# Value slabs first, query and key slabs in pairs behind them: one edit to the head of a two-block transformer kernel

## The chip, the cores and the metric

The kernel runs on one core of a Trainium2 chip. The metric is the device time of one execution in microseconds (us), as the median of several runs. The core has five engines: TensorE (PE, matmuls), VectorE (DVE), ScalarE (ACT), GpSimd (POOL) and SyncE (SP). Each works through its own instruction stream in order and waits on semaphores for the others. SyncE and ScalarE also issue DMAs, each on its own queue.

## The reference

Two transformer blocks in fp32 on 512 tokens of 1024 features. What matters here is the first block's head: a norm, one wide projection, and its retention half.

```python
h = rmsnorm(x, norm_mix[l])
p = h @ w_in[l]
y_ret = retention_mixer(p[..., :RET_PROJ], ...)      # q, k, v, gate: 512 columns each
y_rwkv = rwkv7_mixer(p[..., RET_PROJ:], ...)

def retention_mixer(p, positions, gn_w, gn_b):
    q, k, v, g = jnp.split(p, 4, axis=-1)
    q = rope(q.reshape(B, S, RET_HEADS, HEAD_DIM), positions)
    k = rope(k.reshape(B, S, RET_HEADS, HEAD_DIM), positions) * (HEAD_DIM ** -0.5)
    y = retention_chunkwise(q, k, v)                 # 8 heads of 64
    return silu(g) * head_group_norm(y, gn_w, gn_b, GN_EPS_RET)
```

## The kernel before, in words

**Slabs.** All weights are cut into slabs of 128 x 1024 values (512 KB). Slab `s` is loaded into `w_raw`, four slots used in turn; SyncE issues the load of slab s + 4 when slab s is done. ScalarE copies it to a rounded `w_hi` (`split_hi`), GpSimd takes the rest, `w_lo = w_raw - w_hi`, and TensorE makes three matmuls for each product: high by high, high by low, low by high. `w_hi` has two slots, so the split of slab s + 2 waits until slab s is done. The input `x` is split in the same way into `a_hi` (ScalarE) and `a_lo` (VectorE), eight feature tiles of 128 (index `kc`).

**Two kinds of slab.** A feature slab (`slab`, L1388 ff.) holds 128 output features over all eight `kc`: 24 matmuls of 128 x 512 into one PSUM bank, banks 0 and 1 in turn. It may begin when the tile two slabs back has been taken out of its bank (`begin`, semaphore `tile_taken`). A value slab (`wide`) holds two `kc` of all 512 value features: also 24 matmuls, twelve for each `kc`, into four banks with tokens on the partitions. Its sums are complete with the fourth of them only.

**Order before.** Slabs 0 to 3 are the query tiles, 4 to 7 the key tiles (`S_RQ`, `S_RK`), 8 to 11 the values (`S_RV`), 12 and on (`S_WA`) the second mixer's projections. Only slab 0 waits for `a_lo` piece by piece. Behind slab 0 TensorE sums the squares of `x` over the features (L1482, L1484: two fp32 matmuls with a tile of ones); ScalarE takes the root, VectorE the reciprocal `rstd`, with which every tile is multiplied when it is taken. Behind slab 4 eight tiny matmuls (L1487) turn `rstd` into a column for the value tiles.

**What a query or key tile needs.** VectorE takes tile j (`qk <- banks, rstd`). ScalarE issues four DMAs that copy it with its halves swapped into `rot` (`swap_halves`). VectorE makes three pieces of `rope`: `tmp <- rot, sin`, `qk <- qk, cos`, `qk <- qk, tmp`. ScalarE copies two halves rounded (`ret_hi`, into `q_twice` or `k_stack`), VectorE subtracts them (`ret_lo`, into `q_low` or `qk_lo`), and ScalarE issues two DMAs that stack the halves on the other partitions (`ret_stack`). In the loops over slabs, at slab s VectorE does: take s, `rope(s - 1)`, `ret_lo(s - 3)`. ScalarE does: `split_hi(s + 2)`, `swap_halves(s)`, `ret_hi(s - 3)`, `ret_stack(s - 4)`. During slabs 8 to 11 VectorE takes nothing until all four are done; it finishes `rope(7)` and the last `ret_lo` there and then takes four value tiles.

**The heads.** Behind each of slabs 12 to 19 TensorE computes `scores(h)` of one head; `scores(h)` for h >= 1 waits until VectorE has multiplied the scores of head h - 1 by the decay (`masked_scores`, tile `s_ret`). Head 0 waits for all eight tiles to be stacked. Behind heads 2, 4, 6 the outputs of a pair of heads are formed (`ret_out`, L1431). The decay table (2 MB) is loaded by a DMA of ScalarE's queue at slab 8.

The instruction streams are written out by hand in these loops; nothing else orders them. The lines L831 to L868 and L401, L338 are helpers that record VectorE's, ScalarE's and GpSimd's pieces.

## Time and profile before

| what | value |
|---|---|
| time, median of 3 runs | 1326.78 us (1326.47 to 1327.30) |
| the profiled execution: its time, its span | 1326.74 us, 1325.0 us |
| TensorE busy in the span | 1264.7 us, 95% |
| VectorE, ScalarE, GpSimd busy | 711.0, 545.7, 533.5 us |
| mean granted clock of TensorE | 0.987 |
| TensorE busy in the first 43.6 us | 29.5 us |
| TensorE busy from 43.6 to 110.2 us | 64.8 us |

The span runs from the first to the last instruction of the profiled execution. "Granted clock" is the share of TensorE's full 2.4 GHz that it was given; its other level is 1.2 GHz, shown as 0.50. A matmul's end is modelled in the profile, so the distance between two starts tells its pace better than its length. The releaser of a wait is inferred from semaphore events.

### The profile page before, as it was taken

How to read it: one execution, taken by the hardware profiler on the slowest of the kernel's cores; microseconds unless marked ns; L12 is line 12 of the kernel's file. 1: busy time of each engine (PE TensorE's matmuls, PEld its weight loads, DVE VectorE, ACT ScalarE, POOL GpSimd, SP SyncE). 2: the span in 40 equal slices, each digit the busy share in tenths (PEclk: the TensorE clock that was granted, in tenths of full speed). 3: DMA queues.
4: the chain of work that ended last, by engine and by line, in shares of the span. 5: the costliest groups of instructions: out<-in, count | busy, mean ns of one | idle time of the engine just before them, and what ended most of it. 6: DMA issues, size and time to landing. Idle time of an engine off the chain costs nothing.

```text
span 1325.0 us, 20731 instructions
## 1 busy us (share of the span) xinstructions
PE 1264.7 (95%) x8300; PEld 1003.5 (76%) x8300; DVE 711.0 (54%) x827; ACT 545.7 (41%) x734; POOL 533.5 (40%) x245
## 2 busy tenths in 40 slices
PE   5999999888899999999999999999999999999995
PEld 3777757677777877788888888888776777777873
DVE  8788756757559533336224143144477755442833
ACT  5332253244253433543223122235332468885342
POOL 4443222710157742274444444445443332223453
PEclk9999999989899999999999999999999999999998
DMA  6571111110045221122223332222422322112221
GB/s 218 160 229 64 64 48 53 59 35 4 12 158 163 100 78 51 48 96 96 95 95 96 101 102 100 96 96 96 144 88 80 108 75 65 64 65 67 99 90 64
DMA packets 35098, 119.91 MB, mean 91 GB/s; under 512 B 4544, under 2 KB 4672, under 8 KB 34624
## 3 DMA queue, kind: packets, MB, share of 16 engines
q1 hardware_dynamic: 29808, 105.78, 24.0%
q10 hardware_dynamic: 5200, 12.85, 3.1%
q8 instruction: 66, 1.08, 0.3%
q14 instruction: 24, 0.20, 0.1%
HBM read 111.01 MB, written 2.10 MB: 85 GB/s over the span
## 4 chain that ended last, share of the span: by engine, by line
PE 78%; DVE 14%; ACT 4%; issue 2%; ACTq 1%; DMA 1%; POOL 0%; DVEq 0%; SPq 0%
PE banks L1383 20%; PE banks L1385 19%; PE banks L1384 19%; DVE y_mid L831 2%; DVE tmp L831 1%; PE banks L1846 1%; PE banks L1404 1%; PE banks L1862 1%; PE banks L1406 1%; PE banks L1405 1%; PE banks L1951 1%; DVE qk L831 1%; PE banks L1936 1%; PE banks L1611 1%; DVE yk L831 1%
## 5 line engine op out<-in xcount | busy, mean ns | idle before, releaser
L338 POOL TENSOR_TENSOR w_lo<-w_raw,w_hi 128x1024 fp32r<-128x1024 f32 x145 | 353.7, 2440 | 536.9 <-ACT w_hi L401 536.7
L401 ACT ACTIVATE w_hi<-w_raw 128x1024 fp32r<-128x1024 f32 x145 | 153.9, 1062 | 333.2 <-PE banks L1385 213.1
L1383 PE MATMUL banks<-a_hi,w_hi 128*128 128x512 f32 x584 | 235.2, 403 | 15.5 <-DVE a_lo L839 13.4
L1385 PE MATMUL banks<-a_hi,w_lo 128*128 128x512 f32 x616 | 241.1, 391 | 0.0
L1384 PE MATMUL banks<-a_lo,w_hi 128*128 128x512 f32 x584 | 228.5, 391 | 0.0
L1385 PE MATMUL banks<-b_hi,w_lo 128*128 128x512 f32 x384 | 149.5, 389 | 0.0
L1383 PEld LDWEIGHTS banks<-a_hi,w_hi 128*128 128x128 f32 x584 | 110.1, 188 | 50.2 <-issue 17.8
L1385 PEld LDWEIGHTS banks<-a_hi,w_lo 128*128 128x128 f32 x616 | 116.2, 189 | 24.9
L831 DVE TENSOR_TENSOR x_res<-banks,x_res 128x512 f32<-128x512 f32 x56 | 38.7, 692 | 178.5 <-PE banks L1385 178.3
L338 POOL TENSOR_TENSOR w_lo<-w_raw,w_hi_mlp 128x1024 fp32r<-128x1024 f32 x36 | 87.3, 2425 | 107.7 <-ACT w_hi_mlp L401 107.7
L1384 PEld LDWEIGHTS banks<-a_lo,w_hi 128*128 128x128 f32 x584 | 110.3, 189 | 21.6 <-issue 0.7
L1383 PE MATMUL banks<-b_hi,w_hi 128*128 128x512 f32 x256 | 101.5, 396 | 0.0
L1384 PE MATMUL banks<-b_lo,w_hi 128*128 128x512 f32 x256 | 99.6, 389 | 0.0
L1385 PE MATMUL banks<-m_hi,w_lo 128*128 128x512 f32 x256 | 99.6, 389 | 0.0
L1385 PEld LDWEIGHTS banks<-b_hi,w_lo 128*128 128x128 f32 x384 | 72.1, 188 | 15.0
L401 ACT ACTIVATE w_hi_mlp<-w_raw 128x1024 fp32r<-128x1024 f32 x36 | 38.2, 1062 | 67.3 <-DMA w_raw<-in_weights 66.9
L401 ACT ACT_TABLE_LOAD x48 | 61.6, 1283 | 8.8 <-DVE qk L831 1.6
L401 ACT ACTIVATE m_hi<-m_mid 128x512 fp32r<-128x512 f32 x32 | 20.3, 634 | 98.6 <-DVE m_mid L839 98.6
L831 DVE TENSOR_TENSOR m_mid<-banks,rstd 128x512 f32<-128x512 f32 x32 | 22.1, 692 | 64.9 <-PE banks L1385 64.7
L1383 PEld LDWEIGHTS banks<-b_hi,w_hi 128*128 128x128 f32 x256 | 48.1, 188 | 10.8 <-issue 1.0
L1384 PEld LDWEIGHTS banks<-b_lo,w_hi 128*128 128x128 f32 x256 | 48.1, 188 | 10.8 <-issue 1.0
L1385 PEld LDWEIGHTS banks<-m_hi,w_lo 128*128 128x128 f32 x256 | 48.0, 188 | 10.1
(372 smaller groups left out, 2389.5 us busy)
## 6 DMA issues: line engine op xcount, KB each, us to landing
w_raw<-in_weights SPq DMA_DIRECT2D x189, 512.0 KB, 3.3
x_in<-in_x SPq DMA_DIRECT2D x4, 512.0 KB, 6.7
rot<-qk ACTq DMA_DIRECT2D x32, 64.0 KB, 2.1
decay<-in_decay ACTq DMA_DIRECT2D x1, 2048.0 KB, 8.9
x_res<-in_x ACTq DMA_DIRECT2D x4, 512.0 KB, 5.5
out_fm<-x_res SPq DMA_DIRECT2D x8, 256.0 KB, 2.1
consts<-in_consts SPq DMA_DIRECT2D x1, 1209.0 KB, 12.0
q_twice<-q_twice ACTq DMA_DIRECT2D x8, 128.0 KB, 3.6
```

The costliest lines, as they stand in the source:

```text
L338: nc.gpsimd.tensor_tensor(o, a, b, op).then_inc(S(name), 1)
L401: return nc.scalar.activation(o, a, f, **kw)
L831: return nc.vector.tensor_tensor(o, a, b, op)
L1383: mm(o, high[:, w], hi[:, kc, :], start=kc == first, stop=False)
L1384: mm(o, high[:, w], lo[:, kc, :], start=False, stop=False)
L1385: done = mm(o, w_lo[:, s % 4, w], hi[:, kc, :], start=False, stop=kc == last)
L1404: mm(o, hi[:, kc, c], high[:, w], start=kc == 0, stop=False)
L1405: mm(o, lo[:, kc, c], high[:, w], start=False, stop=False)
L1406: last = mm(o, hi[:, kc, c], w_lo[:, s % 4, w], start=False, stop=kc == KC - 1)
L1611: last = mm(place(2 * f + p, u, 2 * h + tp), ABR[r, f, h, t, 0, :], X[r, f, h, t, :], start=True, stop=True)
L1846: last = mm(o, xq[:, 2 * h + d, t * P:(t + 1) * P], mem_k[:, 2 * h + d, :], start=d == 0, stop=d == 1)
L1862: last = mm(psum[6 + d][:], mem_v[:, m, h * MEM + d * P:h * MEM + (d + 1) * P], prob_t[:, h % 2, m, :], start=m == 0, stop=m == 1)
```

## The change

The value slabs become slabs 0 to 3 and wait for `a_lo` at each `kc`. The sum of squares stands behind slab 2, the eight tiny matmuls stay behind slab 4. Query and key tiles are slabs 4 to 11 in the order query 0, key 0, query 1, key 1 and so on (`head_tile`), so that heads 0 and 1 need only the first two of them; each pair of heads now waits for its own stacks (`q_stacked0` to `q_stacked3`) and its own `q_lo`. VectorE takes the four value tiles behind its second query-key tile. With i = s - 4, ScalarE's `ret_hi` and `ret_stack` stand one slab earlier after their tile than before, and the `decay` load is at slab 6. `rope(7)` and the last three `ret_lo` go to slabs 12 to 14. GpSimd squares two feature tiles of `x` instead of three, behind slab 1's `w_lo` instead of slab 0's, and ScalarE six instead of five. ScalarE splits slab 1 ahead of the last four `a_hi`. The trigonometric steps stand before the reciprocal.

```diff
-N_POOL_SQ = 3
+N_POOL_SQ = 2
-S_RQ, S_RK, S_RV = 0, 4, 8
+S_RV, S_QK = 0, 4
@@ ScalarE
             for kc in range(KC):
                 x_hi(kc)
-            split_hi(1)
+                if kc == 3:
+                    split_hi(1)
...
             for s in range(S_MK):
                 split_hi(s + 2)
-                if 1 <= s < S_RV:
-                    swap_halves(s)
-                if 3 <= s < 11:
-                    ret_hi(s - 3)
-                if 4 <= s < 12:
-                    ret_stack(s - 4)
+                i = s - S_QK
+                if 0 <= i < 8:
+                    swap_halves(i)
+                if 2 <= i < 10:
+                    ret_hi(i - 2)
+                if 3 <= i < 11:
+                    ret_stack(i - 3)
@@ VectorE
+            for s in range(S_QK, S_MK):
+                i = s - S_QK
+                if i < 8:
+                    tt(qk[:, head_tile(i), :], bank[:], rstd[:], ALU.mult).then_inc(D("tile_taken"), 1)
+                    if i >= 1:
+                        rope(i - 1)
+                    if i >= 3:
+                        ret_lo(i - 3)
+                    if i == 1:
+                        dve.wait_ge(S("column_done"), 1)
+                        cp(r_tok[:], psum[6][:, 0:8]).then_inc(D("column_ready"), 1)
+                        for t in range(TT):
+                            ts(v_ret[:, t, :], psum[2 + t][:], r_tok[:, 2 * t:2 * t + 1], None, ALU.mult).then_inc(D("tile_taken"), 1)
...
+                    if s == S_WA:
+                        rope(7)
+                    if s < S_WA + 3:
+                        ret_lo(s - S_WA + 5)
@@ TensorE
-                if s == 0:
+                if s == 2:
                     pe.wait_ge(S("x_sq_pool"), 2 * N_POOL_SQ - 1)
                     mm(psum[7][:], C("ones"), sq_in[:, 0, :], start=True, stop=False)
...
+                    if h % 2 == 0:
+                        pe.wait_ge(S("q_lo_ready"), 2 * h + 4)
+                        pe.wait_ge(S(f"q_stacked{h // 2}"), 4 * 16)
                     if h == 0:
-                        pe.wait_ge(S("q_lo_ready"), 16)
-                        pe.wait_ge(S("q_stacked"), 16 * 16)
```

TensorE's stream at the start of the program, before the change: the last matmuls of slab 0, the two of the sum, the first of slab 1. In these rows the names are tiles, and `consts` holds the ones.

```order
L1383 MATMUL banks<-a_hi,w_hi 128x512 [waits a_lo_ready]
L1384 MATMUL banks<-a_lo,w_hi 128x512
L1385 MATMUL banks<-a_hi,w_lo 128x512
L1482 MATMUL banks<-sq_in,consts 128x512 [waits x_sq_pool]
L1484 MATMUL banks<-sq_in,consts 128x512 [waits x_sq_sum]
L1383 MATMUL banks<-a_hi,w_hi 128x512 [waits w_lo_ready]
```

And TensorE's stream in the changed kernel, across the join of slab 0 (its last three matmuls, in value form) and slab 1.

```order
L1414 MATMUL banks<-w_hi,a_hi 128x512
L1415 MATMUL banks<-w_hi,a_lo 128x512
L1416 MATMUL banks<-w_lo,a_hi 128x512
L1414 MATMUL banks<-w_hi,a_hi 128x512 [waits a_lo_ready,w_lo_ready]
L1415 MATMUL banks<-w_hi,a_lo 128x512
L1416 MATMUL banks<-w_lo,a_hi 128x512
```

The sum has left the place behind slab 0, and the wait for `a_lo` stands once in twelve matmuls instead of once in three.

VectorE's stream around slab 12 before the change: the last value tiles, slab 12's tile with its shift and mix, and the first masked scores.

```order
L835 TENSOR_SCALAR v_ret<-banks,small 128x512 [waits q_lo_ready,slab_done]
L835 TENSOR_SCALAR v_ret<-banks,small 128x512 [waits tile_taken] x3
L831 TENSOR_TENSOR shift<-banks,rstd 128x512 [waits tile_taken,slab_done]
L831 TENSOR_TENSOR tmp<-shift 128x512 [waits tile_taken]
L839 SCALAR_TENSOR_TENSOR low<-tmp,params,shift 128x512 [waits dve_step]
L843 CAST spread_r<-consts 128x1024 [waits low_ready,masks_loaded]
L831 TENSOR_TENSOR s_ret<-banks,decay 128x512 [waits dve_step,s_ret_done,decay_loaded]
```

VectorE's stream at the same place in the changed kernel.

```order
L842 TENSOR_TENSOR shift<-banks,rstd 128x512 [waits q_lo_ready,slab_done]
L842 TENSOR_TENSOR tmp<-shift 128x512 [waits tile_taken]
L850 SCALAR_TENSOR_TENSOR low<-tmp,params,shift 128x512 [waits dve_step]
L842 TENSOR_TENSOR tmp<-rot,sin_r 128x512 [waits low_ready,rot_loaded1]
L842 TENSOR_TENSOR qk<-qk,cos_r 128x512 [waits dve_step]
L842 TENSOR_TENSOR qk<-qk,tmp 128x512 [waits dve_step]
L842 TENSOR_TENSOR qk_lo<-qk,k_stack_79 64x512 [waits rope_done,q_hi_ready]
L842 TENSOR_TENSOR qk_lo<-qk,k_stack_80 64x512 [waits q_lo_ready,q_hi_ready]
L854 CAST spread_r<-consts 128x1024 [waits q_lo_ready,masks_loaded]
L842 TENSOR_TENSOR s_ret<-banks,decay 128x512 [waits dve_step,s_ret_done,decay_loaded]
```

The value tiles have left the place ahead of slab 12's tile, and a whole `rope` and a `ret_lo` stand between it and the first masked scores.

## Rows read from the trace of the kernel before

**Rows 1.** The page, part 1: busy us (share of the span) and instructions.
```profile
PE 1264.7 (95%) x8300; PEld 1003.5 (76%) x8300; DVE 711.0 (54%) x827; ACT 545.7 (41%) x734; POOL 533.5 (40%) x245
```

**Rows 2.** Who TensorE waited for: us in total, times, longest.
```profile
PE banks L1383 <- DVE a_lo L839: 13.4, 4, 10.5
```

**Rows 3.** TensorE in time: start us, us, line, operation, [idle before <-releaser].
```profile
10.47 0.76 PE L1383 MATMUL banks<-a_hi,w_hi 128*128 128x512 f32 x1 [10.47 <-DVE a_lo L839]
...
15.39 0.40 PE L1384 MATMUL banks<-a_lo,w_hi 128*128 128x512 f32 x1
...
22.94 1.91 PE L1482 MATMUL banks<-sq_in,consts 128*128 128x512 f32 x2
...
25.71 0.80 PE L1383 MATMUL banks<-a_hi,w_hi 128*128 128x512 f32 x1
...
48.93 1.05 PE L1487 MATMUL banks<-consts,rstd 1*128 1x2 f32 x8
...
49.91 0.50 PE L1383 MATMUL banks<-a_hi,w_hi 128*128 128x512 f32 x1
...
55.49 0.39 PE L1383 MATMUL banks<-a_hi,w_hi 128*128 128x512 f32 x1
```

**Rows 4.** Start of the program: VectorE, then ScalarE, same columns.
```profile
8.47 13.21 DVE L839 SCALAR_TENSOR_TENSOR a_lo<-x_in,params,a_hi 128x512 fp32r<-128x512 f32 x8 [2.78 <-ACT a_hi L401]
...
15.33 3.29 ACT L401 ACTIVATE sq_in<-x_in 128x512 f32<-128x512 f32 x5
```

**Rows 5.** VectorE over one slab, then the GpSimd piece beside it.
```profile
51.25 0.69 DVE L831 TENSOR_TENSOR qk<-banks,rstd 128x512 f32<-128x512 f32 x1
52.04 2.45 DVE L831 TENSOR_TENSOR tmp<-rot,sin_r 128x512 f32<-128x512 f32 x1
...
56.05 1.48 DVE L831 TENSOR_TENSOR q_low<-qk,q_twice 64x512 fp32r<-64x512 f32 x2
57.63 0.69 DVE L831 TENSOR_TENSOR qk<-banks,rstd 128x512 f32<-128x512 f32 x1
...
51.55 2.40 POOL L338 TENSOR_TENSOR w_lo<-w_raw,w_hi 128x1024 fp32r<-128x1024 f32 x1 [4.08 <-ACT w_hi L401]
```

**Rows 6.** ScalarE queue and engine behind a stacking step, then GpSimd.
```profile
84.95 1.16 ACTq L471 DMA_DIRECT2D k_stack<-qk_lo  x2
86.23 1.06 ACT L401 ACTIVATE w_hi<-w_raw 128x1024 fp32r<-128x1024 f32 x1 [4.54 <-DVE qk_lo L831]
...
87.37 2.40 POOL L338 TENSOR_TENSOR w_lo<-w_raw,w_hi 128x1024 fp32r<-128x1024 f32 x1 [4.58 <-ACT w_hi L401]
```

**Rows 7.** A VectorE piece that GpSimd runs into, and that GpSimd piece.
```profile
75.43 1.48 DVE L831 TENSOR_TENSOR qk_lo<-qk,k_stack 64x512 fp32r<-64x512 f32 x2
...
76.61 2.56 POOL L338 TENSOR_TENSOR w_lo<-w_raw,w_hi 128x1024 fp32r<-128x1024 f32 x1 [3.28 <-ACT w_hi L401]
```

**Rows 8.** VectorE: value slabs taken, slab 12, first masked scores; then TensorE.
```profile
91.21 3.11 DVE L835 TENSOR_SCALAR v_ret<-banks,small 128x512 f32<-128x512 f32 x4
95.91 0.69 DVE L831 TENSOR_TENSOR shift<-banks,rstd 128x512 f32<-128x512 f32 x1 [1.59 <-PE banks L1385]
...
101.07 2.07 DVE L831 TENSOR_TENSOR s_ret<-banks,decay 128x512 f32<-128x512 f32 x4
...
103.19 0.50 PE L1417 MATMUL banks<-q_twice,k_stack 128*128 128x512 f32 x1 [0.58 <-DVE s_ret L831]
```

**Rows 9.** DMA issues of two stretches (76.2 and 77.4): KB, us to landing.
```profile
decay<-in_decay ACTq DMA_DIRECT2D x1, 2048.0 KB, 8.9
...
k_stack<-qk_lo ACTq DMA_DIRECT2D x1, 128.0 KB, 8.7
```

**Rows 10.** Stretches: busy PE, PEld, DVE, ACT, POOL, clock, DMA.
```profile
22.00:25.40 3.40, 3.34 (x6) 1.52 (x6) 2.97 (x5) 0.00 (x0) 0.00 (x0) 0.50 0.30 75
...
257.00:261.00 4.00, 0.10 (x4) 0.10 (x8) 3.66 (x5) 0.00 (x0) 4.00 (x4) 0.99 0.01 4
...
261.00:264.30 3.30, 3.07 (x65) 2.29 (x66) 2.59 (x3) 0.00 (x0) 3.30 (x2) 0.50 0.01 2
```

More of the change, by code:

```diff
@@ L265, in hybrid_blocks, with qk_taken, head_tile @@
         y_lo = at("y_lo", 78, [P, KC, T], F32R)
+        def qk_taken(i):
+            return i + 1 if i < 2 else S_QK + i + 1
+        def head_tile(i):
+            return i // 2 + NF * (i % 2)
         def t4(a):
@@ L462, in ret_hi, with ret_stack @@
                     actv(ret_part(j, k)[r], qk[r, j, :], copy).then_inc(A("q_hi_ready"), 1)
-            def ret_stack(j):
-                act.wait_ge(S("q_lo_ready"), 2 * j + 2)
-                act.wait_ge(S("q_hi_ready"), 2 * j + 2)
+            def ret_stack(i):
+                j = head_tile(i)
+                act.wait_ge(S("q_lo_ready"), 2 * i + 2)
+                act.wait_ge(S("q_hi_ready"), 2 * i + 2)
                 for k in range(2):
@@ L470, in ret_stack @@
                     src = ret_part(j, k)[r] if j < NF else qk_lo[r, j, :]
-                    act.dma_start(ret_part(j, k)[other].bitcast(F32), src.bitcast(F32)).then_inc(S("q_stacked"), 16)
+                    act.dma_start(ret_part(j, k)[other].bitcast(F32), src.bitcast(F32)).then_inc(S(f"q_stacked{i // 2}"), 16)
             def silu(f):
@@ L885, in _, with rope, ret_lo @@
             step(ts(trig[:, 3, :], trig[:, 2, :], -magic, None, ALU.add))
+            step(stt(trig[:, 1, :], trig[:, 3, :], -c1, trig[:, 1, :], ALU.mult, ALU.add))
+            step(stt(trig[:, 1, :], trig[:, 3, :], c1 - two_pi, trig[:, 1, :], ALU.mult, ALU.add))
+            ts(trig[:, 0, :], trig[:, 1, :], -3.1415925, 3.1415925, ALU.max, ALU.min).then_inc(D("angle_ready"), 1)
             dve.wait_ge(S("rms_ready"), 1)
             recip(rstd[:], rstd[:]).then_inc(D("rstd_ready"), 1)
-            def rope(j):
-                dve.wait_ge(S(f"rot_loaded{j % 2}"), 16 * 4 * (j // 2 + 1))
-                step(tt(tmp[:, 0, :], rot[:, j % 2, :], sin_r[:], ALU.mult))
+            dve.wait_ge(S("sines_ready"), 1)
+            step(tt(trig[:, 2, :], trig[:, 1, :], trig[:, 1, :], ALU.mult))
+            step(ts(cos_r[:], trig[:, 2, :], -2.0, 1.0, ALU.mult, ALU.add))
+            def rope(i):
+                j = head_tile(i)
+                dve.wait_ge(S(f"rot_loaded{i % 2}"), 16 * 4 * (i // 2 + 1))
+                step(tt(tmp[:, 0, :], rot[:, i % 2, :], sin_r[:], ALU.mult))
                 step(tt(qk[:, j, :], qk[:, j, :], cos_r[:], ALU.mult))
                 tt(qk[:, j, :], qk[:, j, :], tmp[:, 0, :], ALU.add).then_inc(D("rope_done"), 1)
-            def ret_lo(j):
+            def ret_lo(i):
+                j = head_tile(i)
                 for k in range(2):
                     r = slice(HD * k, HD * k + HD)
-                    dve.wait_ge(S("q_hi_ready"), 2 * j + k + 1)
+                    dve.wait_ge(S("q_hi_ready"), 2 * i + k + 1)
                     high = q_twice[k][r, j, :] if j < NF else k_stack[k][r, j - NF, :]
@@ L1363, in _ @@
             mm = nc.tensor.matmul
-            wide_slabs = set(range(S_RV, S_WA)) | set(range(S_MV, S_WOUT)) | set(range(S_VIN, S_V2))
+            wide_slabs = set(range(S_RV, S_QK)) | set(range(S_MV, S_WOUT)) | set(range(S_VIN, S_V2))
             def begin(s):
@@ L1372, in begin @@
                 if before >= 0:
-                    pe.wait_ge(S("tile_taken"), before + 1)
+                    pe.wait_ge(S("tile_taken"), qk_taken(before - S_QK))
             def part(s, hi, lo, kcs, ready=None, k=0, at=0, first=0, last=KC - 1):
@@ L1471, in _ @@
             for s in range(S_MK):
-                if S_RV <= s < S_WA:
-                    if s == S_RV:
-                        pe.wait_ge(S("column_ready"), 1)
+                if s < S_QK:
                     i = s - S_RV
-                    wide(s, a_hi, a_lo, (2 * i, 2 * i + 1), (4, 5, 6, 7))
+                    wide(s, a_hi, a_lo, (2 * i, 2 * i + 1), (2, 3, 4, 5), "a_lo_ready")
                 else:
-                    slab(s, a_hi, a_lo, "a_lo_ready" if s == 0 else None)
-                if s == 0:
+                    slab(s, a_hi, a_lo)
+                if s == 2:
                     pe.wait_ge(S("x_sq_pool"), 2 * N_POOL_SQ - 1)
@@ L2091, in lay_out @@
     rw = 2048
-    s = slabs(w_in[:, 0:1024]) + wide(w_in[:, 1024:1536])
+    s = wide(w_in[:, 1024:1536]) + slabs(w_in[:, 0:1024].reshape(DM, 2, NF, P).transpose(0, 2, 1, 3).reshape(DM, 1024))
     s += slabs(w_in[:, rw + 1536:rw + 1792]) + slabs(np.concatenate([w_in[:, rw + 1792:], pad], axis=1))
```

65 lines of the change are left out of this document (22 added, 43 removed).

## The prediction, made before the changed kernel was run

> **What bounds the kernel now.** TensorE is busy 95% of the span [rows 1], so I looked first for the places where it isn't. The view of who waited for whom has one large entry: 13.4 us behind VectorE's `a_lo` pieces, 10.5 of them before the first matmul [rows 2]. The time order of TensorE shows the rest of it: slab 0 starts at 10.47, the sum of squares at 22.94, slab 1 at 25.71 [rows 3]. A slab in the steady state takes 5.4 to 5.6 us (slab 5: 49.91 to 55.49), 0.23 us a matmul. So slab 0 and the sum take 15.2 us for about 7 us of work. The second view is VectorE from slab 1 on. One slab costs it 6.38 us (51.25 to 57.63), more than TensorE's 5.44, and 1.76 of that is a piece of 0.69 us that takes 2.45: it ends 0.54 us behind GpSimd's `w_lo` piece (51.55 + 2.40) [rows 5]. TensorE hardly feels this before the change, since the four value slabs follow (some 22 us in which VectorE takes no tile) and VectorE is idle for 1.6 us ahead of slab 12's result [rows 8]. The change spends exactly that reserve.
>
> **The head, a gain.** Each `a_lo` piece takes VectorE 1.65 us on average [rows 4] (13.21 / 8). A feature slab eats three matmuls (0.7 us) for one, a value slab twelve (2.7 us), so TensorE no longer waits for `a_lo`. Slab 0 starts at 10.47 as before. The pace there is 0.43 us a matmul, and it is 0.23 from about 15.3 [rows 3]; I keep that, as TensorE is no less busy: 11 matmuls to 15.3, 13 more to 18.3, slab 1 to 23.75. Slab 2 needs `w_lo` of slab 2. ScalarE does eight `a_hi` pieces (6.4 from 7.7), `w_hi` of slab 1 (1.1), six squares (6 x 0.66, [rows 4]): 19.3 without any wait for slab 1's load, which moves ahead of four `a_hi`; that load had landed by about 14.2, since its split of 1.1 stands ahead of the squares at 15.33, so the wait is 0 to 3.3; I take the middle, 21.0. Then `w_hi` and `w_lo`, 1.1 and 2.4 [rows 6]: 24.7, a wait of 1 us. Slab 2 ends at 30.3. The two sum matmuls took 2.77 with the clock at 0.50 [rows 3, 10]; at the full clock I take half, 1.4. The five adds and the two GpSimd squares are hidden under slabs 1 and 2, the root, its reciprocal and the sines under slabs 3 and 4 (10.9 us). Slab 3 ends at 37.15, slab 4 at 42.6, the eight small matmuls cost 0.98 [rows 3], slab 5 starts at 43.6, where before it is 49.91: **6.3 us ahead**. If nothing else were late this would be the whole result.
>
> **The pairs, VectorE and ScalarE.** From slab 5 on (done at 49.45) I walk VectorE. Tile 1 with the first rope and one held piece (0.79 + 2.26 + 1.8), the copy and the four value pieces, now here (3.11, [rows 8]): 57.95. They read PSUM and one column, so GpSimd doesn't hold them. Tile 2 and its rope: 61.1. Tile 3: its rope needs `rot` of tile 2, which ScalarE can issue only behind the take at 58.8, and 2.5 us after the 2 MB `decay` load, now issued at about 55.6 on the same queue. That load took 8.9 us, and a 128 KB DMA issued 1.2 behind it 8.7 [rows 9]. So `rot` lands at 65 to 67, beside GpSimd's piece (63.9 to 66.3), and tile 3 ends at 69.9.
>
> From there on a loop is closed that was open. `ret_stack(i - 3)` stands in ScalarE's queue ahead of the next slab's `w_hi`, and it now waits for `ret_lo(i - 3)`, VectorE's last piece of the same slab (before: of the slab before it). Behind it are queued `w_hi`, so `w_lo`, so TensorE, and the next swap. From the end E of a VectorE slab: stacking issue 1.16 us, `w_hi` at E + 1.3, `w_lo` at E + 2.45 [rows 6]. VectorE by then has taken the tile and is at its fourth piece (E + 2.34). Its work without GpSimd is 6.38 - 1.76 = 4.62. Bounds of the hold: GpSimd 0.16 late (as in [rows 7], 2.56 for 2.40, where they meet for 0.3 us), 1.7, so 6.35 a slab; GpSimd waits for the whole fourth piece, 2.1, so 6.75; GpSimd first, holding the fourth piece and what follows, 2.4, so 7.0. I take **6.7**. TensorE's slab s + 2 can begin at E + 5.3 or so, so TensorE now waits in this stage, about 3.5 us before slab 10 and under 1 us before slabs 9, 11 and 12; alone that would cost nothing, as VectorE is later still. Slabs 8 to 11: VectorE ends tile 7 at 69.9 + 4 x 6.7 = 96.7. TensorE is through slab 12 at about 94.
>
> The Trainium skill (SBUF — State Buffer, Who interferes with whom) says that of a VectorE instruction with two SBUF inputs and a GpSimd one that reads SBUF, whoever starts first holds the shared ports for its whole length and the other one stands. By it the fourth piece, 0.11 us ahead, would push GpSimd back in full: 6.75 a slab, and the sum would be 0.2 us higher. The trace agrees on the order of who stands, and has no case of so long an overlap.
>
> **Slab 12 and scores(1), the loss.** Before the change VectorE needs 7.23 us from the take of slab 12 (95.91) to the last `s_ret` piece (101.07 + 2.07) [rows 8], and TensorE waits 0.58 us for it ahead of `scores(1)` at 103.19. Now `rope(7)` and `ret_lo(5)` stand in between, 4.62 - 0.79 = 3.83 more, and the start is 96.7: 96.7 + 7.23 + 3.83 = 107.8. TensorE is at that wait at about 100.8 (slab 12, scores(0), slab 13), idle for 7 us. **103.19 becomes 107.8: 4.6 us later.** The two `ret_lo` left (slabs 13 and 14) have 8 us of TensorE a slab beside them, and their stacks are asked for before heads 4 and 6 only; I price them at 0. Behind this point TensorE has no wait that could take up the delay.
>
> **The clock.** TensorE idle for 4 us at 257 to 261 was followed by 3.3 us at 0.50 [rows 10]. A gap of 7 us should do the same: 3.3 us at half the pace lose 1.7; at the start the low level lasted 4.8 us from the first matmul [rows 3], a loss of 2.4. I take 2.0, with 0 to 3.4 as bounds. The low stretch of before at 22 to 25.4 goes (counted above); one behind the gap at slab 10 is likely and hidden behind VectorE.
>
> **Sum.** The profiled execution took 1326.74 us (span 1325.0 and 1.7 around it), the median is 1326.78; I add to the latter. Head -6.3, given back and 4.6 more at scores(1): +4.6; clock +2.0. **1326.8 + 6.6 = 1333.4 us.** Own range: at best 4 x 6.35 and no low clock, +3.2 less 0.3 for a shorter tail, 1329.7; at worst 4 x 7.0, `rot` 0.6 later, clock 3.4, +9.8, and now and then a `rot` that lands late, 1337.5.
>
> **Rivals.**
> 1. The head's gain stays, 1320.5 us. This needs VectorE to be through its first `s_ret` by about 96.7, the end of slab 13 in a run without waits: 49.45 + 47.3. The walk has 58.4. It would hold if GpSimd didn't hold VectorE at all (7 holds of 1.7 to 2.1, 13 us); every steady piece of [rows 5, 8] speaks against that. Chance 0.07.
> 2. The walk is right in kind but TensorE's delay is small: holds at 6.35 or less, `rot` not late, no low clock: 1326 to 1329.4. For it: ScalarE's waits vary, and the four value pieces can cover a GpSimd piece. Chance 0.11.
> 3. A `rot` DMA that meets a 512 KB slab load lands late twice or more, each time holding the rope and so the whole loop for 1 to 2 us: 1336 to 1339. Chance 0.10.
> 4. The change doesn't bring its head gain, because `w_lo` of slab 2, or slab 1's load, is late by 3 us. All of the walk shifts with it: 1336. Chance 0.06.
> 5. The forecast, 1329.4 to 1336: 0.66.
>
> About 0.2% (2.65 us) is what a measurement of this kernel can tell from no change. Slower by more than that is 3, 4 and 5 together, 0.82; within it 0.10; faster 0.08. The range of 8 in 10 goes from 1328.7 to 1337.5.
>
> **What would show it.** Right: slab 5 starts at about 43.6; TensorE's waits for `a_lo` shrink to the first one and those for `w_lo` grow to 5 us or more over slabs 9 to 12; `w_hi` pieces of these slabs wait for VectorE's `q_low` and `qk_lo`; `scores(1)` starts near 107.8 with an idle of 6 to 7 us behind `s_ret`, and the clock reads 0.5 behind it. Wrong: no wait at `scores(1)`, or VectorE at 5.5 us a slab in slabs 8 to 11; then it is rival 1. If slab 5 starts later than 45, the head was misjudged.

## The result, and the profile after

The changed kernel takes 1339.98 us as the median of five runs (1337.33 to 1340.79), the kernel before 1326.78 us in the same series. The ratio is 1.0098, with a 95% interval of 1.0087 to 1.0109: slower by 13.2 us. The forecast of 1333.4 us had the direction and half the size, and the measured time lies above the range that it gave (1328.7 to 1337.5). The profiled execution of the changed kernel took 1337.33 us (span 1335.5 us), just inside that range; it is the fastest of its five.

The page, part 1, of the changed kernel: busy us (share of the span) and instructions. It answers to [rows 1].

```profile
PE 1266.0 (95%) x8300; PEld 1005.3 (75%) x8300; DVE 710.0 (53%) x828; ACT 545.8 (41%) x735; POOL 533.9 (40%) x243
```

TensorE has the same work, 1266.0 against 1264.7 us. So some 9 of the 10.5 us by which the span grew are waiting (busy time also holds what a low clock stretches). Whom it waits for, of the changed kernel (us in total, times, longest), answers to [rows 2].

```profile
PE banks L1414 <- DVE a_lo L850: 9.8, 1, 9.8
...
PE banks L1391 <- POOL w_lo L346: 6.8, 2, 6.0
PE banks L1427 <- DVE s_ret L842: 6.7, 1, 6.7
...
PE banks L1414 <- POOL w_lo L346: 3.1, 2, 1.7
```

The four waits for `a_lo` have become one, as the change intends, 13.4 us before and 9.8 after. Two waits are new in size. The one for `s_ret` was 0.58 us [rows 3, 8] and is 6.7. The one for `w_lo` in the feature slabs holds 6.0 us at one place.

TensorE in time, changed kernel, to be laid beside [rows 3] and the last row of [rows 8]: start us, us, line, operation, [idle before <- releaser].

```profile
25.23 0.50 PE L1414 MATMUL banks<-w_hi,a_hi 128*128 128x512 f32 x1 [1.74 <-POOL w_lo L346]
...
30.80 1.02 PE L1490 MATMUL banks<-sq_in,consts 128*128 128x512 f32 x2
...
32.12 0.80 PE L1414 MATMUL banks<-w_hi,a_hi 128*128 128x512 f32 x1
...
44.51 0.50 PE L1391 MATMUL banks<-a_hi,w_hi 128*128 128x512 f32 x1
...
79.07 0.80 PE L1391 MATMUL banks<-a_hi,w_hi 128*128 128x512 f32 x1 [6.01 <-POOL w_lo L346]
...
111.50 0.80 PE L1427 MATMUL banks<-q_twice,k_stack 128*128 128x512 f32 x1 [6.67 <-DVE s_ret L842]
```

Slab 2 starts at 25.23, slab 5 at 44.51, slab 10 at 79.07, `scores(1)` at 111.50. The head is 5.4 us ahead of before (49.91 - 44.51), and 67 us later the kernel is 8.3 us behind (111.50 - 103.19).

VectorE in between, same columns. It is the view in which the loss is made.

```profile
58.82 0.69 DVE L842 TENSOR_TENSOR qk<-banks,rstd 128x512 f32<-128x512 f32 x1
...
61.87 0.69 DVE L842 TENSOR_TENSOR qk<-banks,rstd 128x512 f32<-128x512 f32 x1
70.05 0.69 DVE L842 TENSOR_TENSOR tmp<-rot,sin_r 128x512 f32<-128x512 f32 x1 [7.49 <-DMA rot<-qk]
...
73.88 0.69 DVE L842 TENSOR_TENSOR qk<-banks,rstd 128x512 f32<-128x512 f32 x1
...
83.50 3.49 DVE L842 TENSOR_TENSOR q_low<-qk,q_twice 64x512 fp32r<-64x512 f32 x2
...
100.38 0.69 DVE L842 TENSOR_TENSOR shift<-banks,rstd 128x512 f32<-128x512 f32 x1
...
109.38 2.06 DVE L842 TENSOR_TENSOR s_ret<-banks,decay 128x512 f32<-128x512 f32 x4
```

Tiles 2 and 3 are taken at 58.82 and 61.87. Then VectorE stands for 7.49 us, until the last of the four DMAs that make the rotated copy of tile 2 has landed. From 73.88 on it takes a tile every 6.63 us, until slab 12's at 100.38, and 11.06 us later the last `s_ret` piece is done (109.38 + 2.06).

Behind the gap the clock falls. A window of the changed kernel: busy us (instructions) of PE, PEld, DVE, ACT, POOL, then clock, DMA share, GB/s.

```profile
111.50:117.60 6.10, 6.10 (x17) 5.13 (x18) 5.60 (x8) 0.63 (x2) 1.73 (x1) 0.50 0.04 10
```

TensorE runs 6.1 us at 1.2 GHz, which loses 3.05 us against 2.4 GHz. `scores(2)` starts at 123.55, where before it is 112.44: 11.1 us later, of which 8.3 were there at `scores(1)`. From there to the end the difference changes by 0.6 us only (the span is 10.5 us longer).

### The profile page after: what moved, and what is told of

Its sections match the earlier page's. It is cut to its first block, busy times and chain, and to the rows that moved or that the text cites. A ratio compares the mean times of both kernels' runs of the same rounds, so it can differ in the third digit from the quotient of the medians.

```text
span 1335.5 us, 20737 instructions
## 1 busy us (share of the span) xinstructions
PE 1266.0 (95%) x8300; PEld 1005.3 (75%) x8300; DVE 710.0 (53%) x828; ACT 545.8 (41%) x735; POOL 533.9 (40%) x243
## 4 chain that ended last, share of the span: by engine, by line
PE 77%; DVE 15%; ACT 4%; issue 2%; DMA 1%; POOL 0%; SPq 0%; DVEq 0%; ACTq 0%
PE banks L1391 20%; PE banks L1392 19%; PE banks L1393 19%; DVE y_mid L842 2%; DVE qk L842 2%; PE banks L1857 1%; PE banks L1414 1%; PE banks L1873 1%; PE banks L1416 1%; PE banks L1415 1%; PE banks L1962 1%; PE banks L1947 1%; DVE AKR L842 1%; DVE tmp L842 1%; DVE X L842 1%
## 5 line engine op out<-in xcount | busy, mean ns | idle before, releaser
L1391 PEld LDWEIGHTS banks<-a_hi,w_hi 128*128 128x128 f32 x584 | 110.7, 190 | 40.9 <-POOL w_lo L346 10.7
L409 ACT ACTIVATE w_hi_mlp<-w_raw 128x1024 fp32r<-128x1024 f32 x36 | 38.2, 1061 | 66.7 <-DMA w_raw<-in_weights 66.2
L842 DVE TENSOR_TENSOR m_mid<-banks,rstd 128x512 f32<-128x512 f32 x32 | 22.1, 692 | 66.2 <-PE banks L1393 66.0
## 6 DMA issues: line engine op xcount, KB each, us to landing
decay<-in_decay ACTq DMA_DIRECT2D x1, 2048.0 KB, 10.9
```

Source lines behind the costliest of these rows:

```text
L409: return nc.scalar.activation(o, a, f, **kw)
L842: return nc.vector.tensor_tensor(o, a, b, op)
L1391: mm(o, high[:, w], hi[:, kc, :], start=kc == first, stop=False)
```

## The experiments

All kernels are made from the changed kernel, but for the second one shown, which is made from the kernel before. Each is timed against runs of the kernel before in its own series, whose median was 1325.75, 1326.87 or 1326.48 us. Times are compared as ratios to it; the brackets are 95% intervals. The changed kernel itself, run again in the last series, is at 1.0094.

### Where the 7.5 us at tile 3 come from: the place of the decay load

**The decay load moved up**, from slab 6 to slab 1 of ScalarE's queue, long before the first swap (and the 256 KB `w0` load with it, to slab 3).

```diff
-                if s == S_QK + 2:
-                    act.dma_start(w0[:], ins["w0"]).then_inc(S("decay_loaded"), 16)
+                if s == 1:
                     act.dma_start(decay[:], ins["decay"]).then_inc(S("decay_loaded"), 16)
+                if s == 3:
+                    act.dma_start(w0[:], ins["w0"]).then_inc(S("decay_loaded"), 16)
```

> The changed kernel with the 2 MB decay load issued by ScalarE behind slab 1's turn instead of behind slab 6's, and the small w0 load behind slab 3's. Nothing else moves. Theory A (VectorE's chain from tile 1 to the first masked scores sets scores(1), and TensorE only waits for it): the rotation DMAs of tile 2 no longer queue behind 2 MB, the idle of 7.5 us before VectorE's third rope shrinks to the 3.5 to 4 us that GpSimd's piece there costs anyway, and scores(1) comes 3.5 us earlier, at about 108.0 instead of 111.5. The low clock behind the gap stays. Time 3.5 us under the changed kernel, about 1336. Rival B (the loop of ScalarE's stacking, the split and TensorE sets the pace, VectorE is late only because it is fed late): the wait comes back in the next slabs, the time stays within 1 us of 1340.

Measured: 1334.62 us, ratio 1.0058 [1.0041, 1.0074], some 4.8 us better than the changed kernel (each of the two intervals reaches some 2 us to either side). `scores(1)` starts at 109.57, 1.9 us earlier where 3.5 was expected, and `scores(2)` 2.2 us earlier, so the trace bears out about half of the 4.8. The wait is halved, not gone. DMA issues of the stretch 56 to 63.5 us in the changed kernel and of 57 to 63 in this one: KB each, median us to landing. Then VectorE of this one at tile 3.

```profile
decay<-in_decay ACTq DMA_DIRECT2D x1, 2048.0 KB, 10.9
w_raw<-in_weights SPq DMA_DIRECT2D x2, 512.0 KB, 6.3
...
rot<-qk ACTq DMA_DIRECT2D x4, 64.0 KB, 6.2
```

```profile
w_raw<-in_weights SPq DMA_DIRECT2D x1, 512.0 KB, 4.7
rot<-qk ACTq DMA_DIRECT2D x4, 64.0 KB, 3.5
```

```profile
61.78 0.69 DVE L843 TENSOR_TENSOR qk<-banks,rstd 128x512 f32<-128x512 f32 x1
66.30 2.53 DVE L843 TENSOR_TENSOR tmp<-rot,sin_r 128x512 f32<-128x512 f32 x1 [3.82 <-DMA rot<-qk]
```

A 64 KB rotation behind the decay load takes 6.2 us in the median, and 3.5 without it, where it still meets a slab load. It now lands beside a GpSimd piece, which holds the rope for 1.84 us (2.53 for 0.69). So the load accounts for 3.75 of the 7.5 us at this place (70.05 - 66.30), of which the GpSimd piece takes half back.

The rope needs all four copies of a rotation, and the median hides the one that counts. In the changed kernel the first three are issued at 59.54, 60.43 and 60.99 and land at 65.7, 66.2 and 67.1. The fourth is issued right behind a slab load of SyncE. The two issues, and their time to landing:

```profile
61.30 0.33 SPq L333 DMA_DIRECT2D w_raw<-in_weights  x1
61.63 0.61 ACTq L460 DMA_DIRECT2D rot<-qk  x1
```

```profile
w_raw<-in_weights SPq DMA_DIRECT2D x1, 512.0 KB, 8.5
rot<-qk ACTq DMA_DIRECT2D x1, 64.0 KB, 8.4
```

It lands at 70.0, 0.2 us behind the slab load (69.8). With the decay load early the same slab load takes 4.7 us and lands at 65.9, and the fourth copy at 66.3. As the rows read, both loads bear on the 7.5 us: the slab load takes longer beside the 2 MB, and the last copy lands with the slab load. No run has the decay load at slab 6 without a slab load beside the copies, so how the wait divides between the two is not shown.

**The same load, moved in the kernel before**, from slab 8 to slab 5. Nothing else of the change is in this kernel.

```diff
-                if s == S_RV:
+                if s == 5:
                     act.dma_start(w0[:], ins["w0"]).then_inc(S("decay_loaded"), 16)
                     act.dma_start(decay[:], ins["decay"]).then_inc(S("decay_loaded"), 16)
```

> The kernel before the change, with its decay load issued by ScalarE at slab 5 instead of slab 8, ahead of three rotations. This prices the load by itself, in the old order. Theory A: the rotation of tile 5 or 6 lands 3 to 5 us late, VectorE waits that long before one rope, and the wait for slab 8's or 9's w_lo grows; VectorE's reserve in slabs 8 to 11 takes most of it, 0 to 3 us over the kernel before. Rival (the late rotation in the changed kernel came from the slab loads alone, not from the 2 MB): no wait before a rope over 2 us.

Measured: 1337.16 us, ratio 1.0083 [1.0061, 1.0104]. That is 10.7 us slower than before from this one move, far above both expectations. Its rows: DMA issues of 57 to 65 us, VectorE, GpSimd, TensorE.

```profile
rot<-qk ACTq DMA_DIRECT2D x6, 64.0 KB, 10.2
```

```profile
70.27 2.60 DVE L831 TENSOR_TENSOR tmp<-rot,sin_r 128x512 f32<-128x512 f32 x1 [6.08 <-DMA rot<-qk]
```

```profile
82.45 2.35 POOL L338 TENSOR_TENSOR w_lo<-w_raw,w_hi 128x1024 fp32r<-128x1024 f32 x1 [10.12 <-ACT w_hi L401]
```

```profile
84.85 0.79 PE L1404 MATMUL banks<-w_hi,a_hi 128*128 128x512 f32 x1 [6.73 <-POOL w_lo L338]
```

The chain can be read off: the rotation lands late (6.08 us), so VectorE's tiles are late by as much, so ScalarE, whose queue holds the next swap and the stacking ahead of the weight split, issues `w_hi` late, so `w_lo` waits 10.12 us and TensorE 6.73 at slab 10, and behind that gap its clock reads 0.50 until 89.7. `scores(1)` starts at 111.08 here, within 0.5 us of the changed kernel. In the kernel before, the load is issued at 76.2, and the last swap ahead of it at 70.9: the load comes behind the last rotation. Two stacking copies are behind it (8.7 us to landing [rows 9]), and nobody waits for them before slab 12. The load's place is an independent part of the change, and taken alone it costs nearly as much as the whole.

### What stands ahead of scores(1)

**The masked scores ahead of the last rope.** Work that only heads 6 and 7 need is put behind that for `scores(1)`; `rot` gets a place in SBUF of its own, since the masked scores would overwrite it.

```diff
-        rot = at("rot", 52, [P, 2, T])
+        rot = at("rot", 152, [P, 2, T])
...
-                    if s == S_WA:
-                        rope(7)
-                    if s < S_WA + 3:
-                        ret_lo(s - S_WA + 5)
...
                     masked_scores(s - S_RET)
+                    if s == S_WA:
+                        rope(7)
+                    if s < S_WA + 3:
+                        ret_lo(s - S_WA + 5)
```

> The changed kernel with one change on VectorE: behind slabs 12 to 14 the masked scores stand ahead of rope(7) and of the three last ret_lo, instead of behind them. The rotation buffer lies elsewhere, since the scores' buffer shared its place. Theory A: the first masked scores end at about 105.6 instead of 111.4, scores(1) waits under 1 us, the clock doesn't fall there (3 us), and 1 to 3 us come back as a wait of ret_out(0) for the second masked scores, since the work is only moved back. Time 5 to 8 us under the changed kernel, 1332 to 1335. Rival B: TensorE's delay was built up in slabs 9 to 12 already, the time falls by 2 us at most. Rival C (the low clock is an own cost of the long gap at slab 10, not of the one at scores(1)): the clock's low stretch behind slab 13 stays.

Measured: 1329.51 us, ratio 1.0028 [1.0019, 1.0038], the largest gain of a single edit, 8.8 us (5 to 8 were expected). TensorE of this kernel:

```profile
105.39 0.50 PE L1427 MATMUL banks<-q_twice,k_stack 128*128 128x512 f32 x1 [0.79 <-DVE s_ret L842]
```

`scores(1)` starts 6.1 us earlier (111.50 - 105.39). Of that the work itself is 3.83 us and the hold of a rope piece by GpSimd some 2.0 (104.14, 2.73 us instead of 0.69, in the changed kernel). The gap shrinks to 0.79 us and there is no low clock behind it: `scores(2)` starts at 114.72, 8.8 us earlier.

**The gap filled.** 24 matmuls of 128 x 512 that nobody reads stand ahead of `scores(1)`, to part the price of the clock from that of the wait.

```diff
+                    if h == 1:
+                        for n in range(24):
+                            mm(psum[7][:], a_hi[:, 0, 0:P], a_hi[:, n % KC, :], start=True, stop=True)
                     scores(h)
```

> The changed kernel with 24 more matmuls of 128 x 512, whose result nobody reads, on TensorE between slab 13 and scores(1), in the gap of 6.7 us. Theory A with the clock as its last term: scores(1) starts where it did, at 111.5, the clock doesn't fall behind it, and the 3.1 us lost at half pace come back: 3 us under the changed kernel, about 1337. If the low clock costs nothing (rival: VectorE is late behind scores(1) too), the time stays.

Measured: 1335.88 us, ratio 1.0068 [1.0051, 1.0085], about 3.4 us under the changed kernel. TensorE and two windows of this kernel:

```profile
106.12 5.60 PE L1511 MATMUL banks<-a_hi 128*128 128x512 f32 x24
113.01 0.50 PE L1427 MATMUL banks<-q_twice,k_stack 128*128 128x512 f32 x1 [1.29 <-DVE s_ret L842]
```

```profile
26.60:30.00 3.40, 3.40 (x9) 2.64 (x9) 3.19 (x3) 0.00 (x0) 1.30 (x1) 0.50 0.00 0
113.00:117.60 4.60, 4.59 (x22) 3.93 (x23) 4.26 (x5) 0.64 (x2) 1.75 (x1) 1.00 0.00 0
```

From `scores(1)` to `scores(2)` it takes 9.26 us, against 12.05 in the changed kernel and 9.25 before. So the low clock behind the gap costs 2.8 us there, in executions that are like the profiled one. In the changed kernel's second series the profiled execution lost about 1.4.

### The loop: ScalarE, GpSimd, VectorE

**Only the value tiles moved**, one slab earlier (behind tile 0, not tile 1).

```diff
-            return i + 1 if i < 2 else S_QK + i + 1
+            return i + 1 if i < 1 else S_QK + i + 1
...
-                    if i == 1:
+                    if i == 0:
                         dve.wait_ge(S("column_done"), 1)
```

> The changed kernel with the four value tiles taken one slab earlier, behind the first query tile, where VectorE is idle for 6 us, instead of behind the second. This takes 3.3 us of work out of VectorE's chain. Theory A with the decay load as its next link: the third rope then waits for a rotation that still lands behind the 2 MB, at about 68 to 70, so nearly all of it is lost: 0 to 1.5 us under the changed kernel. If the load were no link, it would be 3.3 us. Rival B: 0.

Measured: 1337.2 us, ratio 1.0079 [1.0059, 1.0099], 2 us better by the medians, but its interval holds the changed kernel's 1.0094: the two can't be told apart. VectorE of this kernel:

```profile
55.25 0.69 DVE L842 TENSOR_TENSOR qk<-banks,rstd 128x512 f32<-128x512 f32 x1 [0.42 <-PE banks L1393]
...
69.47 0.69 DVE L842 TENSOR_TENSOR tmp<-rot,sin_r 128x512 f32<-128x512 f32 x1 [8.09 <-DMA rot<-qk]
```

VectorE is 3.6 us earlier at tile 2, and all but 0.6 of it is spent in the wait for the rotation. Its fourth copy is issued 3.2 us earlier than in the changed kernel (58.43) and lands 0.6 earlier, again behind the slab load. The place of the value tiles only counts once that wait is gone.

**The loop opened.** `ret_hi` and `ret_stack` stand one slab later in ScalarE's stream, as they did before the change.

```diff
-                if 2 <= i < 10:
-                    ret_hi(i - 2)
-                if 3 <= i < 11:
-                    ret_stack(i - 3)
+                if 3 <= i < 11:
+                    ret_hi(i - 3)
+                if 4 <= i < 12:
+                    ret_stack(i - 4)
```

> The changed kernel with ret_hi and ret_stack of each tile one slab later in ScalarE's queue, as they stood before the change, so that no split of weights waits for VectorE's last piece of the same slab. Theory A: TensorE's wait before slab 10 shrinks from 6.0 us, its waits for w_lo in slabs 9 to 12 to under 2 us together, but scores(1) still waits for VectorE. VectorE's slab goes from 6.6 to about 6.4 us, five times, so about 1 us earlier: 0 to 2 us under the changed kernel. Rival B: all of these waits come off the time, 6 to 8 us.

Measured: 1338.08 us, ratio 1.0085 [1.0068, 1.0102]: no difference that can be told from the changed kernel. What TensorE waits for did change, and the start of `scores(1)` did not.

```profile
74.99 0.47 PE L1391 MATMUL banks<-a_hi,w_hi 128*128 128x512 f32 x1 [3.38 <-DVE qk L842]
...
83.42 0.50 PE L1391 MATMUL banks<-a_hi,w_hi 128*128 128x512 f32 x1 [1.11 <-POOL w_lo L346]
```

The wait for `w_lo` before slab 10, 6.01 us in the changed kernel, is gone and has become one for VectorE; `scores(1)` is at 111.25 and waits 9.9 us there instead of 6.7. The split of weights was not what set the start of `scores(1)`. VectorE was.

**GpSimd's piece cut** to 128 of 1024 columns in slabs 7 to 14; TensorE's low product reads those 128 columns eight times there.

```diff
-                    mul(w_lo[:, s % 4, :], w_raw[:, s % 4, :], hi_slot(s)[0].bitcast(F32), "w_lo_ready", ALU.subtract)
+                    n = P if 7 <= s <= 14 else KC * P
+                    mul(w_lo[:, s % 4, 0:n], w_raw[:, s % 4, 0:n], hi_slot(s)[0][:, 0:n].bitcast(F32), "w_lo_ready", ALU.subtract)
...
-                    done = mm(o, w_lo[:, s % 4, w], hi[:, kc, :], start=False, stop=kc == last)
+                    done = mm(o, w_lo[:, s % 4, slice(0, P) if 7 <= s <= 14 else w], hi[:, kc, :], start=False, stop=kc == last)
```

> The changed kernel with GpSimd's low part of slabs 7 to 14 made for 128 of 1024 columns, which TensorE then reads eight times, so these slabs' low parts are left out of the product; the matmuls are as many and as large. It takes the GpSimd piece from 2.4 us to about 0.35 and with it the hold of VectorE. Theory A: VectorE's slab goes from 6.6 to about 4.7 us, the wait for the late rotation stays, scores(1) starts at 102 to 103 instead of 111.5, time 9 to 12 us under the changed kernel, 1328 to 1331. If the hold by GpSimd were no link of the chain (rival D: VectorE's slab is long because it waits for ScalarE's copies), the slab stays above 6 us and the time falls by 2 us at most.

Measured: 1331.86 us, ratio 1.0044 [1.0027, 1.0061]. VectorE of this kernel:

```profile
73.81 0.69 DVE L843 TENSOR_TENSOR qk<-banks,rstd 128x512 f32<-128x512 f32 x1
...
78.50 0.69 DVE L843 TENSOR_TENSOR qk<-banks,rstd 128x512 f32<-128x512 f32 x1
...
81.54 1.56 DVE L843 TENSOR_TENSOR q_low<-qk,q_twice 64x512 fp32r<-64x512 f32 x2
84.67 0.69 DVE L843 TENSOR_TENSOR qk<-banks,rstd 128x512 f32<-128x512 f32 x1 [1.58 <-PE banks L1394]
```

With a GpSimd piece of 0.9 us the two halves of `q_low` take 1.56 instead of 3.49, and a tile 4.69 instead of 6.6. So the hold is 1.9 us of every slab. `scores(1)` starts at 104.80, 6.7 us earlier. That and the time (6.6 us under the changed kernel) are less than expected, since from 84.67 on VectorE waits for TensorE.

### All together, and what then beats both kernels

**The decay load, the masked scores and the value tiles**, the three edits above in one kernel.

> The changed kernel with three of the edits together: the decay load early, the value tiles one slab earlier, the masked scores ahead of rope(7) and the last ret_lo. Theory A: each link of VectorE's chain is now shorter by what it alone could not give. The third rope no longer waits for a late rotation, since its DMAs go out 3 us before the loads of slab 11, so the third tile ends at about 67 instead of 73.8; four slabs of 6.6 us follow, 93.4, and the first masked scores end 5.3 us later, at 98.7 to 99, against 103.1 in the kernel before. Time 3 to 5 us under the kernel before, about 1322. Rival B (the order of slabs itself costs, the closed loop alone gives back the head's gain): not under the kernel before.

Measured: 1324.48 us, ratio 0.9983 [0.9973, 0.9992]. It is 2.3 us faster than the kernel before and 0.0111 (14.7 us) below the changed kernel in ratio; the three single gains add up to 15.6 (4.8 + 8.8 + 2.0, the last within noise). Under the kernel before 3 to 5 us were expected. VectorE at tile 3 and TensorE at `scores(1)`:

```profile
61.42 0.69 DVE L843 TENSOR_TENSOR tmp<-rot,sin_r 128x512 f32<-128x512 f32 x1
62.15 2.77 DVE L843 TENSOR_TENSOR qk<-qk,cos_r 128x512 f32<-128x512 f32 x1
...
67.33 0.69 DVE L843 TENSOR_TENSOR qk<-banks,rstd 128x512 f32<-128x512 f32 x1
```

```profile
99.09 0.50 PE L1428 MATMUL banks<-q_twice,k_stack 128*128 128x512 f32 x1 [0.81 <-DVE s_ret L843]
```

No wait for a rotation, tile 4 is taken at 67.33 rather than 73.88, and `scores(1)` starts at 99.09, 4.1 us ahead of before.

**The same with the loop opened.**

> The three edits together and, in addition, ret_hi and ret_stack one slab later in ScalarE's queue. Theory A: with the loop open TensorE's waits for w_lo shrink, VectorE's slab is 6.4 instead of 6.6 us; 0 to 2 us under the run with the three edits, so 1320 to 1322. Rival: the copies come later for VectorE's ret_lo, which then waits, 0 to 2 us above it.

Measured: 1327.35 us, ratio 1.0002 [0.9991, 1.0013], 2.9 us slower than with the loop closed by the medians. The two were run in one series, and the fastest run of this one (1326.55) is slower than the slowest of the other (1325.53). VectorE and TensorE:

```profile
93.91 2.19 DVE L843 TENSOR_TENSOR tmp<-shift 128x512 f32<-128x512 f32 x1
...
96.99 2.66 DVE L855 CAST spread_r<-consts 128x1024 fp32r<-128x1024 f32 x1
```

```profile
101.91 0.80 PE L1428 MATMUL banks<-q_twice,k_stack 128*128 128x512 f32 x1 [6.37 <-DVE s_ret L843]
```

With weights split early GpSimd runs freely, and two of its pieces meet VectorE on the short way to `s_ret`: 1.5 and 2.0 us of hold. VectorE takes slab 12's tile 0.65 us earlier than with the loop closed (93.18 against 93.83), and the two holds turn that into 2.8 us later. With the loop closed neither piece is held (0.69 and 0.69 us): GpSimd's pieces keep to one place of VectorE's slab.

**The split of slab 2 ahead of four squares**, in the changed kernel, against the 1.74 us at 25.23.

```diff
             for kc in range(N_POOL_SQ, KC):
                 x_squares(kc)
+                if kc == 3:
+                    split_hi(2)
...
             for s in range(S_MK):
-                split_hi(s + 2)
+                if s > 0:
+                    split_hi(s + 2)
```

> The changed kernel with ScalarE's split of slab 2 ahead of its last four squares instead of behind them. Theory A: the wait before slab 2 goes from 1.7 us to under 0.4, no execution has a low clock there, slab 5 starts at 43 instead of 44.5. The third rope waits for the rotation behind the decay load, which is issued off TensorE's slab 6 and moves with it, so all of this comes off the time: 1.5 us under the changed kernel of the same set, up to 3 where that one had the low clock. Rival: the adds of the squares are late for the sum by as much, 0.

Measured: 1336.1 us, ratio 1.0074 [1.0052, 1.0095]. TensorE:

```profile
24.21 0.50 PE L1417 MATMUL banks<-w_hi,a_hi 128*128 128x512 f32 x1 [0.48 <-POOL w_lo L346]
...
43.48 0.50 PE L1394 MATMUL banks<-a_hi,w_hi 128*128 128x512 f32 x1
```

The head gains 1.0 us, and so does everything up to tile 4: the decay load is issued 1.0 earlier, the rotation lands at 69.01 instead of 70.05, tile 4 is taken at 72.84. One later slab takes 7.1 us instead of 6.6, and `scores(1)` at 111.14 shows 0.4 of the gain. By the time alone the kernel can't be told from the changed one.

**All three with this split.**

> The three edits together (decay load early, value tiles one slab earlier, masked scores ahead of the last rope) and the split of slab 2 ahead of the squares. Theory A: 1.5 to 2.5 us under the three edits alone, so 4 to 5 us under the kernel before, about 1322. Rival: at this point TensorE's waits for w_lo in slabs 9 to 12 set the end, and the time stays 2 us under the kernel before.

Measured: 1323.66 us, ratio 0.998 [0.9969, 0.999], 2.8 us faster than the kernel before and not told apart from the three edits alone. `scores(1)` starts at 98.22 and `scores(2)` 4.9 us ahead of before, but the span is 1.9 us shorter only. By the starts of GpSimd's pieces the lead is still 4.8 us at 375 us and 1.8 at 397; in between the clock of this kernel reads 0.66 from 380 to 390, where before it reads 1.00. Such low-clock stretches fall at different places in every execution, of the kernel before too, so I can't say that this edit causes one.

**The changed kernel again**, in the last series.

> The changed kernel itself once more, beside the others of this set, since its runs lay 3.5 us apart (1337.3 to 1340.8). Theory A: the same chain, scores(1) at 111 to 112 and 8 us behind the kernel before. What differs between its executions is the wait before slab 2 (1.7 us in one trace, 2.7 in a trace of its kin) and whether TensorE's clock falls behind it; then slab 5 starts at 46 instead of 44.5. Time 1338 to 1340.

Measured: 1338.6 us, ratio 1.0094 [1.0079, 1.0109]. In its trace slab 5 starts at 44.43, `scores(1)` at 110.95 behind a gap of 6.7 us, `scores(2)` at 121.61.

## Why the prediction had the direction and half the size

**The terms.** In the profiled execution:

| term | forecast | measured |
|---|---|---|
| head: slab 5 | 43.6, -6.3 | 44.51, -5.4 |
| `scores(1)` | 107.8, +4.6 | 111.50, +8.3 |
| clock behind it, to `scores(2)` | +2.0 | +2.8 |
| the rest of the span | 0 | -0.6 |
| profiled execution | +6.6 | +10.6 |
| median | +6.6 | +13.2 |

**The head.** The mechanism is as forecast: one wait for `a_lo`, no sum of squares at the low clock (two matmuls and their step 1.32 us, forecast 1.4). The wait before slab 2 was forecast as 1.0 us and is 1.74. ScalarE reached the split of slab 2 as forecast (21.12, forecast 21.0), but GpSimd's piece behind it took 2.9 us instead of 2.4, and slab 1 was through 0.3 us early, since slab 0 started at 9.77 and not at 10.47. Slab 5 is 0.9 us later than the walk.

**The step that failed** is this one: "So `rot` lands at 65 to 67 [...] and tile 3 ends at 69.9". Three of its four copies did land at 65.7 to 67.1; the fourth, which the rope needs as well, landed at 70.0, and tile 4 was taken at 73.88, 3.98 us late. I had seen half of the mechanism (a swap on the same queue behind the 2 MB load) and priced it from one row, a DMA issued 1.2 us behind the load before the change that took 8.7 us [rows 9]; my worst case had `rot` only 0.6 us later. (The 2.5 us that I put between load and swap don't follow from my own 55.6 and 58.8, which give 3.2; measured 3.3.) Two things were not in the walk. The load itself took 10.9 us here instead of 8.9. And SyncE's slab load at 61.30 stood ahead of the fourth copy, issued at 61.63; I had such a meeting as a rival and not in this sum. The windows of the changed kernel show the DMA engines full from 60 to 70 us.

```profile
60.00:62.00 2.00, 2.00 (x10) 1.65 (x10) 1.83 (x4) 0.00 (x0) 0.00 (x0) 1.00 1.15 492
...
68.00:70.00 2.00, 2.00 (x11) 1.64 (x10) 0.00 (x0) 0.00 (x0) 0.00 (x0) 1.00 0.92 278
70.00:74.00 4.00, 3.06 (x14) 2.20 (x12) 3.57 (x6) 0.00 (x0) 0.00 (x0) 1.00 0.04 14
```

The fourth copy lands when they fall idle, some 2.9 us behind the decay load (56.25 + 10.9 = 67.15, against 70.05). To price it I should have counted all data in flight, of both queues, and not taken the time of another DMA near it. The Trainium skill (DMA: Bandwidth & Descriptors, Queues, rings and completion order) says that on each DMA engine the descriptors of one issuing engine's ring are consumed in order, while rings of different issuers take turns. Landings of whole copies can show that only in part: three copies land before the decay load issued ahead of them is complete, and the next tile's first three, issued 2.2 us and more behind the fourth copy on the same queue, land before it (68.5 to 69.1). So its place in ScalarE's queue alone doesn't explain the fourth, and why just this one lands with the slab load stays open. The experiment in the kernel before puts a size on the load's place: 10.7 us.

**The loop.** Forecast 6.7 us a slab, measured 26.50 / 4 = 6.63. It is the fourth piece and GpSimd that meet, as drawn. GpSimd of the changed kernel, with VectorE's piece of 83.50 above:

```profile
82.80 2.85 POOL L346 TENSOR_TENSOR w_lo<-w_raw,w_hi 128x1024 fp32r<-128x1024 f32 x1 [3.78 <-ACT w_hi L409]
```

The fourth piece starts at 82.71, GpSimd at 82.80 takes 2.85 instead of 2.40, and `q_low` stands 2.01 us (3.49 for 1.48). So the rule of the Trainium skill that the prediction named (whoever starts first holds the shared ports) is borne out in the main: GpSimd's piece grew by 0.45 us where 0.6 of the fourth piece were left, and its 6.75 and the 6.7 taken are both within 0.12 of the measured slab. The trace before did have an overlap of this length, which I had missed: GpSimd's piece at 17.46 took 2.81 us beside an `a_lo` piece that ended at 18.04. The cut GpSimd piece showed the cause: 4.69 us a tile. That ScalarE's queue closes a loop was right as a description (6.01 us before slab 10, forecast 3.5, larger as everything is later there) and harmless, as written: opened, it changed the time by nothing that can be told from noise.

**Slab 12 to scores(1).** Forecast 7.23 + 3.83 = 11.06, measured 109.38 + 2.06 - 100.38 = 11.06. The idle time forecast as 7 us is 6.67. The sum was right with a share of luck: the 7.23 us before held a 2.0 us hold by GpSimd (the `low` piece at 97.37 took 2.77 instead of 0.75), and a 2.04 us hold of a rope piece took its place.

**So +8.3 instead of +4.6** is 3.98 us at tile 3, less 0.3 from the loop. Of the 3.98 about 0.7 are the later head, which moves the decay load (56.25, forecast 55.6), the slab load and the swap with it (the kernel with the early split of slab 2 shows such a shift carried through, 1.0 at slab 5 and 1.0 at tile 4). The other 3.3 are the landing itself. The clock term was taken as 2.0 and measured 2.8. Its upper bound had no row of the clock behind it: at the start of the kernel before the profile's granted clock reads 1.00 from 10 to 15.3 us, and it is the pace (0.43 us a matmul against 0.23) that is low there. `scores(1)` and the clock, 3.7 and 0.8 us over the forecast, less the 0.6 given back later, make 4.0 of the 6.6 us that were missing in the median; the other 2.6 are the distance from the profiled execution to the median, and their cause stays open (below).

**The rivals.** The third (a rotation that meets a slab load and lands late, 1336 to 1339) had the mechanism, and was given a chance of 0.10; it named two or more such landings of 1 to 2 us each, where one, with the decay load in flight as well, did it all. The first (the head's gain stays) fell: VectorE's `s_ret` was the wait. In the kernel with three edits it came true in part: 4.1 us of the head's gain were still there at `scores(1)`, and the end gained 2.3.

**What stays open.** The four other runs of the changed kernel took 1338.9 to 1340.8 us, and the profiled one 1337.3; in the last series 1338.3 to 1339.2 against 1335.6. Some 3 us of the 13.2 are thus in no trace of it. A candidate is the wait before slab 2: in the kernel with the filled gap it is 2.63 us rather than 1.74, the clock reads 0.50 from 26.6 to 30.0 behind it, and slab 5 starts at 46.10, 1.6 us later, as does tile 4 by 1.5 (75.33). The kernel that shortens that wait to 0.48 us has a median no longer than its profiled execution (1336.1 and 1337.1), which fits. But its ratio's interval overlaps that of the changed kernel, and I have no trace of a slower execution of the latter. The kernel with all three edits and the loop opened speaks against it: its wait at that place is 2.73 us, the clock reads 1.00 behind it (26 to 30), and slab 5 starts at 44.80. Low-clock stretches further on, at other places in each execution, are another candidate. So this is argued, not shown.

## What to carry to other kernels

Before a large load is moved, look at what is behind it on its queue and who waits for that: a 2 MB load ahead of pending 64 KB copies cost 11 us against the same load behind the last of them. And look at the last of a group of copies, since the reader waits for all: here it was the one that met a load of the other queue. When a change moves work, find the first wait it feeds (`s_ret` for `scores(1)` here) and put ahead of it only what it needs; that one reordering was worth 8.8 us and needed no engine to be faster. A gain at the head is kept only if the engine that works through the following slabs has slack to use it, and here the slack of VectorE (22 us without tiles) had been spent by the same change.
